# Two-layer streaming encoder trunk: the memory panels' work in another order on VectorE and ScalarE

## The reference

```python
for i in range(2):
    mem_kv = rmsnorm(mem, mem_norm[i]) @ w_mem_kv[i]          # 256 x 1024: keys | values
    u = rmsnorm(h, norm_mix_pre[i])
    if i == 0:
        proj = u @ ssd_w_in                                    # z | x, B, C | dt | memory queries
        y_mix = ssd_mixer(...)                                 # conv, chunked scan, gate by silu(z), rmsnorm
    else:
        proj = u @ swa_w_in                                    # banded attention with sinks
        y_mix = swa_sink_attention(...)
    y_mem = memory_cross_attention(proj[..., -512:], mem_kv)
    h = h + rmsnorm(concatenate([y_mix, y_mem], -1) @ w_out, norm_mix_post[i])
    h = h + rmsnorm(squared_relu_mlp(rmsnorm(h, norm_mlp_pre[i]), w_up[i], w_down[i]), norm_mlp_post[i])
```

## Time and profile before

| | us |
|---|---|
| median of 3 runs (lowest to highest) | 1337.57 (1336.29 to 1338.17) |
| the profiled execution's own time | 1336.79 |
| its span | 1335.1 |
| TensorE busy | 1324.6 (99%) |
| VectorE, ScalarE, GpSimd busy | 687.9, 588.6, 114.5 |
| the memory panels, 246.1 to 313.1 in the span | 67.0 |
| VectorE, ScalarE busy in these | 57.2, 51.0 |

### The profile page before, as it was taken

The page is one execution under the profiler, slowest core; times in us unless marked ns, Lnnn a source line. Parts: engine busy times, 40 slices in busy tenths (PEclk is TensorE's granted clock), DMA queues, the critical chain, the costliest instruction groups (busy, mean ns, idle before and its releaser), DMA issues.

```text
span 1335.1 us, 18387 instructions
## 1 busy us (share of the span) xinstructions
PE 1324.6 (99%) x6935; PEld 1093.5 (82%) x6935; DVE 687.9 (52%) x1080; ACT 588.6 (44%) x1105; POOL 114.5 (9%) x131
## 2 busy tenths in 40 slices
PE   9999999999999999999999999999999999999998
PEld 7778888888788888888888898777898888888886
DVE  5586677887436443223443364875474432244333
ACT  6645455676435443213332344765354322133321
POOL 0044352660000000000000000000000000000000
PEclk9999999999999999999999999999999999999999
DMA  7343433243432323233222233112223323322221
GB/s 221 104 126 100 130 103 102 93 163 112 159 109 80 99 93 108 95 127 95 94 98 92 79 100 119 48 64 80 79 81 102 114 98 110 95 94 95 97 100 72
DMA packets 75551, 137.75 MB, mean 103 GB/s; under 512 B 6342, under 2 KB 16854, under 8 KB 75478
## 3 DMA queue, kind: packets, MB, share of 16 engines
q1 hardware_dynamic: 71184, 134.76, 31.2%
q10 hardware_dynamic: 4294, 2.00, 0.8%
HBM read 133.41 MB, written 2.93 MB: 102 GB/s over the span
## 4 chain that ended last, share of the span: by engine, by line
PE 97%; DVE 1%; DMA 1%; ACT 1%; issue 1%; DVEq 0%; ACTq 0%
PE G L1733 64%; PE X L1733 12%; PE X L1756 7%; PE G L1806 3%; PE X L1806 3%; PE X L1912 1%; PE X L1921 1%; PE X L1995 1%; PE X L2210 1%; PE X L2182 1%; PE X L2200 1%; DMA raw<-in_w_mem_kv 1%; PE X L1934 1%; PE X L1974 1%; PE X L1983 0%
## 5 line engine op out<-in xcount | busy, mean ns | idle before, releaser
L1118 DVE TENSOR_TENSOR wlo<-raw,whi 128x1024 fp32r<-128x1024 f32 x207 | 252.6, 1226 | 441.9 <-ACT whi L567 440.8
L567 ACT ACTIVATE whi<-raw 128x1024 fp32r<-128x1024 f32 x207 | 217.7, 1058 | 421.3 <-PE G L1733 209.7
L1733 PE MATMUL G<-uhi,whi 128*128 128x512 f32 x736 | 294.3, 400 | 0.2 <-DVE ulo L1135 0.2
L1733 PE MATMUL G<-uhi,wlo 128*128 128x512 f32 x736 | 287.1, 390 | 0.0
L1733 PE MATMUL G<-ulo,whi 128*128 128x512 f32 x736 | 286.7, 390 | 0.0
L1733 PEld LDWEIGHTS G<-uhi,whi 128*128 128x128 f32 x736 | 138.2, 188 | 31.2 <-issue 1.1
L1733 PEld LDWEIGHTS G<-uhi,wlo 128*128 128x128 f32 x736 | 138.1, 188 | 29.5 <-DVE wlo L1166 0.2
L1733 PEld LDWEIGHTS G<-ulo,whi 128*128 128x128 f32 x736 | 138.3, 188 | 28.4
L1733 PE MATMUL G<-whi,hidhi 128*128 128x512 f32 x256 | 99.6, 389 | 0.0
L1733 PE MATMUL G<-whi,hidlo 128*128 128x512 f32 x256 | 99.6, 389 | 0.0
L1733 PE MATMUL G<-wlo,hidhi 128*128 128x512 f32 x256 | 99.6, 389 | 0.0
(11 more groups left out here) (342 smaller groups left out, 2240.5 us busy)
## 6 DMA issues: line engine op xcount, KB each, us to landing
raw<-in_w_up SPq DMA_DIRECT2D x64, 512.0 KB, 3.8
raw<-in_w_down SPq DMA_DIRECT2D x64, 512.0 KB, 3.5
raw<-in_ssd_w_in SPq DMA_DIRECT2D x20, 512.0 KB, 3.6
raw<-in_w_mem_kv SPq DMA_DIRECT2D x16, 512.0 KB, 3.6
raw<-in_ssd_w_out SPq DMA_DIRECT2D x16, 512.0 KB, 3.5
raw<-in_swa_w_in SPq DMA_DIRECT2D x16, 512.0 KB, 3.8
raw<-in_ssd_w_in SPq DMA_DIRECT2D x16, 384.0 KB, 3.4
csrow<-cs_rows SPq DMA_DIRECT2D x16, 384.0 KB, 4.4
```

The source lines that it names most:

```text
L567: act.activation(whi[q][:, :, :], raw[q % 2][:, :, :], ACT.Copy).then_inc(hi_done, 1)
L1118: dve.tensor_tensor(wlo[q][:, :, :], raw[q % 2][:, :, :], whi[q][:, :, :].bitcast(F32), ALU.subtract).then_inc(lo_done, 1)
L1733: mm = pe.matmul(o, st, mv, start=(kt == 0 and fresh and not go_on), stop=(q == total - 1 and k == 1), skip_group_check=True)
```

## The change

Four things, all in panels 36 to 51, with not one instruction more or less on any engine's arithmetic:

1. VectorE: `unit_masked` and the six `Kseg` instructions go ahead of the low part, in the unit's own panel p; for a group's first unit the product with the exponential too.
2. ScalarE: for units 13, 14 and 15 the exponential goes from the end of panel p to panel p + 1, behind `y0_hi`.
3. ScalarE: the second half of a block's copy goes ahead of the high part.
4. The second layer's keys take the banks in the order 2, 0, 3, 1 and its values banks 0 and 2, with the waits to match.

```diff
+KEY_BANK = ((0, 1, 2, 3), (2, 0, 3, 1))
+VALUE_BANK = ((0, 1), (0, 2))
+VALUE_FREE = (((2, 0), (3, 1)), ((1, 0), (3, 2)))
+VALUE_WAIT = ((0, 1, 2, 3), (0, 2, 3, 1))
...
@@ ScalarE, panel
-                f = Y0_SLOT.get((p, 0))
-                if f is not None and f < 9:
-                    y0_hi(f)
+                if p in Y0_PANEL:
+                    y0_hi(Y0_PANEL[p])
+                    if p - 1 in UNIT_AT:
+                        unit_exp(UNIT_AT[p - 1])
...
                 if next_panel is not None:
-                    i, j = divmod(p // 4 - B_MEM, 2)
+                    if p % 4 == 3:
+                        mem_copy(*divmod(p // 4 - B_MEM, 2), 1)
                     ahead(*next_panel)
-                    if p % 4 == 3:
-                        mem_copy(i, j, 1)
                 if v is not None:
                     if not ahead_of_hi:
                         unit_turned(v)
-                    unit_exp(v)
+                    if p + 1 not in Y0_PANEL:
+                        unit_exp(v)
...
@@ VectorE, panel
                 v = UNIT_AT.get(p - 1)
-                if v is not None:
-                    unit_within(v)
+                if v is not None and p <= 4 * B_MEM:
+                    unit_segments(v)
+                if v is not None and (p <= 4 * B_MEM or v % NT):
+                    unit_decayed(v)
...
                 v = UNIT_AT.get(p)
-                ahead_of_lo = next_panel is not None and v is not None and v % NT == 0
-                if ahead_of_lo:
+                if v is not None:
                     unit_masked(v)
+                if v is not None and next_panel is not None:
+                    unit_segments(v)
+                    if v % NT == 0:
+                        unit_decayed(v)
                 if next_panel is not None:
                     ahead(*next_panel)
-                if v is not None and not ahead_of_lo:
-                    unit_masked(v)
```

More of the change, by code:

```diff
@@ L83 @@
 Y0_SLOT = {(44 + f, 0): f for f in range(9)} | {(53, 1): 9, (53, 3): 10, (54, 1): 11}
+Y0_PANEL = {44 + f: f for f in range(9)}
 Y0_LO = Y0_SLOT | {(54, 0): 10}
@@ L597, in mem_copy @@
                         group_ready(act, N_MEM + n, 4 * (B_MEM + n) + 4, b)
-                        act.activation(memKT[i][:, b, :], G[b][:, 0:M], ACT.Copy).then_inc(bank_free[b], 1)
+                        o = KEY_BANK[i][b]
+                        act.activation(memKT[i][:, b, :], G[o][:, 0:M], ACT.Copy).then_inc(bank_free[o], 1)
                 else:
@@ L602, in mem_copy @@
                     for x in range(2):
-                        act.activation(memV[i][:, t, M * x:M * x + M], G[t][:, M * x:M * x + M],
-                                       ACT.Copy).then_inc(bank_free[t if x else 2 + t], 1)
+                        act.activation(memV[i][:, t, M * x:M * x + M], G[VALUE_BANK[i][t]][:, M * x:M * x + M],
+                                       ACT.Copy).then_inc(bank_free[VALUE_FREE[i][t][x]], 1)
             act.wait_ge(eps_done, 1)
@@ L1270, in unit_masked, with unit_segments @@
                 dve.tensor_tensor(CBm[:, :], X[2][:, 384:512], upper[:, :], ALU.mult).then_inc(s_cbm, 1)
-            def unit_within(v):
+            def unit_segments(v):
                 g, c = divmod(v, NT)
@@ L1283, in unit_within, with unit_decayed @@
                 k.then_inc(s_k, 1)
+            def unit_decayed(v):
                 dve.wait_ge(s_k, v + 1)
@@ L1847, in tokens_still, with weights_still @@
                 return form
-            def weights_still(x_of):
+            def weights_still(x_of, banks=(0, 1, 2, 3)):
                 def form(b, s, k, kt):
@@ L1853, in form @@
                     cols = slice(P * b, P * b + P)
-                    o = G[b][:, 0:xh.shape[1]]
+                    o = G[banks[b]][:, 0:xh.shape[1]]
                     return [(o, whi[s][:, k, cols], xh, True), (o, whi[s][:, k, cols], xl, False),
@@ L1866, in x_still, with x_still_mem @@
                 return form
-            def x_still_mem(hi_t, lo_t):
+            def x_still_mem(hi_t, lo_t, i):
                 def form(b, s, k, kt):
@@ L1872, in form @@
                         return []
-                    rows, o = slice(P * (b // 2), P * (b // 2) + P), G[b // 2][:, :]
+                    rows, o = slice(P * (b // 2), P * (b // 2) + P), G[VALUE_BANK[i][b // 2]][:, :]
                     return [(o, hi_t[:, kt, rows], whi[s][:, k, :], k == 0),
@@ L2093, in _ @@
                 else:
-                    form = x_still_mem(mhi, mlo) if (blk - B_MEM) % 2 else weights_still(mem_of)
+                    i, j = divmod(blk - B_MEM, 2)
+                    form = x_still_mem(mhi, mlo, i) if j else weights_still(mem_of, KEY_BANK[i])
                     ready = u_wait(U_MEM)
-                free = bank(blk) if blk > 0 else lambda b: pe.wait_ge(ulo_ready, b + 1)
+                if blk == 0:
+                    free = lambda b: pe.wait_ge(ulo_ready, b + 1)
+                elif blk < B_MEM:
+                    free = bank(blk)
+                else:
+                    order = (VALUE_WAIT if j else KEY_BANK)[i]
+                    free = lambda b, n=blk, order=order: pe.wait_ge(bank_free[order[b]], n)
                 gemm(blk, blk, 4, form, ready, free, after_bank=behind_block(blk), first=(blk == 0))
```

## The result

| | before | after |
|---|---|---|
| median of the runs taken side by side (us) | 1336.57 (1336.22 to 1338.17, 20 runs) | 1338.06 (1337.44 to 1341.56, 20 runs) |
| ratio after to before | | 1.0016, 95% interval 1.0009 to 1.0023 |
| the profiled execution, and its span (us) | 1336.79, 1335.1 | 1339.94, 1338.2 |
| panels 36 to 51, first product to first product of panel 52 (us) | 67.04 | 70.21 |

The change made the kernel slower, by 0.16%. That lies under the 0.2% named in the prediction and inside its range, but the forecast was a gain of 1.5 us and the runs show a loss of about that size. The last line of the table, worked out from TensorE's timeline, holds it all: the span without these panels is 1268.1 us before and 1268.0 after.

A forecast was written before the change was run, and what follows sets the result against it. TensorE was taken as the bound, busy 1324.6 of 1335.1 us, with 2.3 us of waits to win. Terms -1.67 - 0.61 + 0.5 + 0.3 gave -1.5 us, 1337.57 to 1336.1 us; range 1334.7 to 1338.4.

The forecast's parts named there:

- Neighbours on GpSimd: Panel 42's low part beside `DI`: would start near 264.7, escape most of `DI`, and end at 266.1 as before.
- the step on unit 12: Scores ahead of panel 44's low part: exponential unmoved, product done by about 273.1, TensorE's 1.67 us wait at `outputs` gone.
- Cost nothing, covered by 0.3 us: Units 10 and 11, panels 36 and 38: panel 41's load 3.8 us later, `xtok` copy still in time for `from_state`.
- The new wait at tile 1: Tile 1's transposes in panel 45: a new TensorE wait of 0.5 us, 1.0 if panel 46's load takes 4.0.
- The exponential: ScalarE's exponential behind tile 1's high part: unit 13's 0.61 us wait at `outputs` goes, with 0.3 us to spare.
- The copies and banks: Second copies ahead of the high part, new bank order: no gain alone, but avoids a bank wait over 2 us in panel 44.
- Near ties: Close timings in units 13 to 15 and for tile 2: cost put at 0.3 us, between nothing and 1.0.
- The sum: Panels 36 to 51: -1.67 - 0.61 + 0.5 + 0.3 = -1.5 us, giving a median of 1336.1 us.
- The wait moving whole: Rival: panel 46's load takes 4.0 and near ties cost 1.0, so no net change, 1337.6 us; chance 0.2.
- The slower rival: `Kseg` beside GpSimd's work doubles, over 2.5 us each in panels 44 to 49, giving 1340.3 us; chance 0.08.

The follow-up runs named there:

- Experiment 3: The change with units 10 and 11's scores back behind the low parts, units 12 to 15 still ahead; 1336.33 us, ratio 0.9996 to the kernel before.
- experiment 4: Kernel before with only the scores of units 10 and 11 put ahead of the low parts; 1336.77 us, ratio 0.9999 to the kernel before.
- experiment 5: The change with GpSimd's `DI` made by six one-input instructions instead of one two-input instruction; 1336.84 us, ratio 1.0003 to the kernel before.
- experiment 12: Only unit 12's scores ahead, its product behind the low part, copies and bank order as before, exponentials moved; 1335.48 us, ratio 0.9991 to the kernel before.
- experiment 7: The change, but on VectorE only unit 12's mask and scores go ahead, its product stays behind the low part; 1334.77 us, ratio 0.9988 to the kernel before.
- experiment 9: The change, but on VectorE only unit 12 moved, its scores and product both ahead of the low part; 1335.91 us, ratio 0.9994 to the kernel before.
- experiment 11: Only unit 12's scores ahead, its product behind the low part, exponentials of units 13 to 15 as before; 1336.01 us, ratio 0.9995 to the kernel before.
- Experiment 6: The change with panel 39's second pair of copies back behind panel 42's high part; 1336.20 us, ratio 1.0000 to the kernel before.
- experiment 8: The change without any edit, one more profile, a single execution; 1336.43 us.
- experiment 10: Only unit 12's scores ahead, its product behind the low part, and `DI` by six one-input instructions; 1334.30 us, ratio 0.9982 to the kernel before.
- experiment 2: The change with part 1 undone, masks and scores as in the kernel before, parts 2 to 4 kept; 1336.14 us, ratio 0.9997 to the kernel before.

## Why the prediction was wrong

**The step that failed is "Neighbours on GpSimd".** It put panel 42's low part at 264.7 in the new order and let it "escape most of" `DI`, ending at 266.1 as before. It moved VectorE's work and left GpSimd's where the old trace had it, `DI` at 263.31, all but past (264.87) when the low part starts. But the same edit, units 10 and 11, also changes what GpSimd's preparations of `csrow` run beside: a group of twelve took 10.45 or 10.46 us in each profile where the scores of units 10 and 11 are late, and 12.53 in the change (12.54 and 11.42 in its other two profiles). That and 0.3 us of later start move `DI` by 2.3 us, so that it lies on the low part again, as it did before. A row of the trace before gave the price, 2.61 us against 1.41; it was used only for the place where it stood. The low part, later and as slow as before, ends at 267.82, 1.7 us later than forecast. So panel 44's load is issued 1.7 us later, its high part starts at 272.01 and not at 270.03, and the exponential, which the step on unit 12 called unmoved at 271.28, starts at 273.25.

**"Cost nothing, covered by 0.3 us" (units 10 and 11) failed with it.** The step did follow panel 41's load, high part and `xtok` copy, and these came as it said (the high part at 257.20, no wait of TensorE at `from_state` of unit 11). It stopped one instruction short: unit 11's exponential behind them, which now waited 1.25 us for GpSimd. Experiment 3 puts units 10 and 11 at 1.4 us, experiment 4 at nothing if the copies stay where they were. Two steps, each costed alone at nothing, cost 1.4 us together.

**Unit 12's 1.67 us: the mechanism was right.** Wherever unit 12's scores go ahead and panel 42's low part ends by 266.6, the wait was gone (experiments 3 and 5 to 12). In experiments 3, 7, 9, 11 and 12 it still meets `DI`, at its old place, and does no harm there; in 5, 6, 8 and 10 it does not.

**The new wait at tile 1: right place, size at its upper end.** Forecast 0.5 us, 1.0 if the load takes 4.0. It measured 1.07 to 1.14 in experiments 3, 8 and 9, where the low part of panel 42 is in time, 1.2 at the longest in 5, and 1.59 and 2.3 with the late meeting. Experiment 6 has none there, but its TensorE had waited for a bank before. The sum took the low part 1.6 us late. In experiment 9 it was 1.72 late and took 1.64 us in the place of 1.41, which is the row that should have been taken.

**The exponential: right.** Undone, it brings back 0.9 us of wait, and 1.1 us in the difference of the medians, 0.8 in the panels (experiment 11 against 7). **The copies and banks: right in kind, too high in size.** The step said over 2 us of bank wait without them; experiment 12 has 1.1. It missed their own price, the 0.5 us by which panel 42's high part is later, called "1 us at most" only for panels 47 and 51. Panel 43, for which the move was made, and panel 39, where it does the harm, are governed by the same line.

**Near ties: one was mis-sized.** The sum gave them 0.3 us, 1.0 at most, with loads of 3.4 to 4.0. Panel 47's load was to land near 280. It was issued 1.9 us behind panel 46's and took 5.4 us, so `from_state` of unit 13 waited 0.67 us. In the other two profiles of the change that load took 4.7 and 4.6 us, and `from_state` did not wait.

**The sum.** With the low part in time the forecast would still have been too good. In experiment 8 the waits are 1.5 us, against 2.3 before, but the panels are only 0.24 us shorter. Set product against product, by their starts, a wait costs more than the view of waits prints, because the modelled end of the product ahead hides some 0.1 to 0.2 us of it. By the starts, experiment 8 gains 1.74 us at unit 12's `outputs` and 0.67 at unit 13's, and loses 1.33 at tile 1, 0.51 at tile 2, 0.13 at unit 13's `from_state` and 0.21 in panel 48. With the late meeting, the change's profiled execution grew by 3.2 us in the panels. By the starts: 0.3 lost at the first products of panel 40, 0.8 gained at unit 12's `outputs`, 1.8 lost at tile 1, 2.6 between unit 13's `from_state` and the products behind its `to_state`, 0.7 gained at unit 13's `outputs`. Of the 2.6, 0.8 are the wait (a start 0.95 us behind the one before, elsewhere 0.12) and 1.7 the half clock.

**The rivals.** The wait moving whole came nearest in its time (1337.6). It named the right resource, the ring of two `raw` buffers, and a wrong cause, a load of 4.0 us for panel 46, which took 3.6. The slower rival was wrong: the longest six `Kseg` took 1.95, 2.29 and 2.24 us in the three profiles of the change, not the 2.5 that it asked for. It had the right neighbour and the wrong pair. The Trainium skill (GPSIMD Engine Reference, section 1, Specifications) says that GpSimd shares its SBUF interfaces with VectorE, with contention for VectorE instructions that have two SBUF inputs. It names no condition on GpSimd's own inputs, and both the low part and `Kseg` have two. The runs agree where GpSimd's instruction has two inputs as well: `DI` stretches the low part to 2.31 to 2.63 us. They do not where it has one: beside such a `DI` the low part takes 1.53 (experiments 5 and 10), against 1.41 alone. Here the measurement decides: the prediction was right to weigh the two kinds of neighbour differently.

**Still open.** Why 31 of 32 executions seem to meet `DI` and one does not: two profiles have it and one has not, for the others only the time speaks. The three part between 252 and 258 us: in the one without it GpSimd's decay of the state took 2.75 us and not 1.21 or 1.22, the twelve preparations 11.42 and not 12.53 or 12.54, and panel 39's low part 1.41 and not 1.98; the exponential came 0.5 us earlier. Why panel 47's load takes longer where it is issued close behind another is open too. Whether the half clock would go if only the waits were spread out was not tried.

## What to carry to other kernels

When an instruction is moved on one engine, move its neighbours on the others too before reading a price from the old trace, and look for every pair that is dear beside each other: here two edits, each free alone, brought such a pair together. Ahead of a step that frees a buffer for a load, put only what fits into the wait that stands there already (the six `Kseg`, 1.67 us into 1.78), and leave behind it whatever waits for someone else (the product, 1.04 us of waiting). Making the dear neighbour cheap to run beside (one-input instructions on a GpSimd with time to spare) shortened the panels by another 0.4 us, though it takes three times as long.

## What the runs showed of the hardware

- A VectorE instruction with two tensor inputs beside one of GpSimd with two: a pair of low-part instructions took up to 2.63 us in the place of 1.41. Beside one-input instructions of GpSimd that cover it whole it took 1.53 (experiments 5 and 10) or 1.64 (the change, at 275.06). GpSimd pays instead: twelve one-input preparations took 10.46 us in one order of VectorE's work and 11.42 to 12.84 in another. Made of six one-input instructions, `DI` took 4.46 and 4.96 us, where the one two-input instruction took 1.56.
- The granted clock of TensorE fell to 0.50, the 1.2 GHz level, for about 3.4 us after waits of 0.86, 1.59 and 0.67 us that ended at 275.20, 283.95 and 285.96, and likewise after 0.65 and 2.31 that ended at 274.93 and 284.41. After a single wait of 1.67 or 1.7 (before, experiment 2), 1.5 in two (experiment 8) or 1.8 in three (experiment 5), it stayed at 1.00. In the change's profile 0.8 us more of waits than before came with 1.7 us lost at the half clock.
- Loads of 512 KB that follow each other closely. Panel 47's load was issued 1.9 us behind panel 46's in all seven profiles with unit 12's product ahead (the change three times, experiments 3, 5, 6 and 9), and took 4.4 to 5.4 us from issue to landing. In the other seven, 3.0 to 4.5 us behind it, it took 3.4 to 3.7. So an order that put these two low parts close together went with a longer second load. That the distance is the cause is not shown: one other load took 4.7 us 3.8 us behind the one before it (experiment 12, issued at 283.7). Panel 43's took 5.2 and 5.3 us in the change, experiments 5 and 6, and 3.8 to 4.2 in the change's other two profiles; what lengthened that one is not known, and it did not bring the loss, since 5 and 6 lack it. All eleven in the change's profile, against 3.4 to 4.0 before:

```profile
DMA to landing us min/median/max: 3.4/3.6/5.4
```
